# Forget rows of the prompt on partitions 0-15 and 64-79, the bias of each pair's odd head contracted over the second set (hybrid RG-LRU, forgetting attention, MoE step)

## The chip, the cores and the metric

One core of a Trainium2 chip runs the whole layer. The metric is device time in microseconds (us) of one execution; the time given is the median of several runs.

## The reference

One step of a decoder layer for two groups of tokens that share the weights: a prompt of 256 tokens and 8 samples of 8 new tokens, each with 256 cached ones. D = 1024, 16 heads of 64, 32 experts, all in fp32.

```
h   = rms_norm(x, g_mix_pre) * (1 + scale1) + shift1        # from c, by w_ada
z   = h @ w_in  ->  x_rnn | q | k | v | f_logit(16) | gate_A | gate_B
A:  causal conv (width 4) -> RG-LRU (block-diagonal gates, scan)
B:  logf = log_sigmoid(f_logit + b_forget);  F = cumsum(logf)      # one row per head
    softmax(q k^T / 8 + F_t - F_s, causal) v
x  += gate1 * rms_norm((sigmoid(gate_A) * A + sigmoid(gate_B) * B) @ w_out)
x  += gate2 * rms_norm(top-4-of-32 SwiGLU experts(...))
```

Outputs are also k, v, logf and the states of both groups. In a softmax row F_t is a constant and falls out, so the kernel adds only -F_s, a row for each head, to the scores.

## The kernel before

It is written with semaphores by hand; each engine has its own list of instructions, in program order.

**Input projection (to about 261 us).** TensorE runs JOBS in order: one job is a block of 128 output rows over all 320 tokens (kinds x, k, v, q, and the gates gb and ga), 8 matmuls over D (L1343), with weights from a staging ring of three chunks of 2 MB. An fp32 matmul shows as two instructions in the trace, so a job is x16. The kinds r and i are the block-diagonal gates (L1338). Kind a is a piece of the adaLN product, in column tiles of 32 (L1326), and a later fold (L1298) adds its four parts up, one job behind. ScalarE evacuates each job (job_ev).

The forget job, kind f, stands between the x and the k jobs. Its weights `wf` (1024 x 16 values) and bias `bfg` are loaded by SP among the small loads (L344, L345), between chunks 6 and 7; its 8 matmuls (L1331) give 16 rows of logits. ScalarE adds the bias (L562), VectorE and ScalarE make log-sigmoid in place (L834 on, `log1p`), a scan along the 256 tokens and a factor -1 give `Fp`, 16 partitions x 256 (L854, L855), and F_made is raised.

**Prompt attention (261 to 378 us).** Heads go in pairs p, 2p on partitions 0-63 and 2p+1 on 64-127 of qT and kT. `scores(p)` writes for two query blocks (128 and 256 keys) the q.k products of both heads (L1387), and adds the bias (L1390): the stationary operand is a column of the identity, broadcast to 128 columns over 16 partitions, which picks head h's row out of `Fp`. The four banks are used as two pairs.

```
for o in range(2):
    row = ident[0:H, 2 * p + o:2 * p + o + 1].to_broadcast([H, 128])
    last = mm(B[2 * (p % 2) + o][:, c:c + n], row, Fp[:, 0:n], start=False, stop=True)
```

TensorE's order is scores(0), scores(1), and then for each p: gate job 2p (L1370, 16 instructions), values(p-1) (L1408, L1411), weights(2p) (three transposes, L1235), gate job 2p+1, weights(2p+1), scores(p+2). VectorE takes the masked maximum and normalizes (L890 to L900), ScalarE does the exponentials (L588, L589).

**Samples and the middle (378 to 535 us).** For each of 8 samples cached keys and values come in (SP, L362), their keys are transposed, and scores and values are made; between them lie output projection, second norm and router.

**Experts (535 us to the end).** 16 pairs of experts; each takes 16 MB of gate-up (L399) and 8 MB of down weights (L403), streamed by SP as the semaphore `used`, which TensorE counts up, frees the slots. The first two transfers wait for the count that TensorE adds ahead of the last two samples (L1575 in the profile).

POOL zeroes and makes masks at the start (L420 to L441), and issues output transfers later.

Of the kernel before, what the change touches and what calls it, by code (L numbers as in the profile page):

```python
# [31 lines left out]
def hybrid_layer(nc, x_prompt, x_sample, cache_k, cache_v, cache_logf, state_conv, state_h, page_table,  # L32
# [11 lines left out]
    NT = D // 128  # L44
# [23 lines left out]
    with ctx:  # L68
# [36 lines left out]
        lfc = fr[:, 2432:2688].rearrange("p (g h) -> p g h", h=H)  # L105
        wf = fr[:, 2688:2816].rearrange("p (k h) -> p k h", h=H)
        onesf = fr[:, 2816:2816 + PAST + DS]
        st36 = fr[:, 3080:3080 + NT * 36].rearrange("p (t c) -> p t c", c=36)
        rs = fr[:, 3368:3688]
        lfcf, lftf = fr[:, 2432:2432 + 272], fr[:, 4008:4096]  # L110
        lfz = fr[0:H, 3688:4008]
        lftok = fr[:, 4008:4056].rearrange("p (t h) -> p t h", h=H)
# [95 lines left out]
        h2S = hf[:, 2048:2560].rearrange("p (m n) -> p m n", m=4)  # L208
        Fp = rs[0:H, 0:SP_]
        Fs = fr[:, 0:2 * (PAST + DS)].rearrange("p (s c) -> p s c", s=2)  # L210
# [5 lines left out]
        sp8, t8, s8, a8 = few(0, 8), few(8, 8), few(16, 8), few(24, 8)  # L216
        bfg = few(32, 1, H)
        brow = few(33, E, 1)
# [24 lines left out]
        def vec(name, n=NT):  # L243
            return vecT[:, V[name]:V[name] + n]


        names = """fold8_made fold_ps silu_zeroed tailk_made sv_ps sv_made smask8_made qsel_made hsel_made smask_made consts_made ident_made x_in rows_in small_in pages_in cachef_in rgw_zeroed rgw_in
            rows_ps vec_made csig_made c_made xT_ps xT_made xT_sq sum_ps ms_made rs_made ada_ps h_made
# [67 lines left out]
        def _(eng):  # L316
# [26 lines left out]
            eng.dma_start(ptab, page_table.rearrange("(o b) g -> o (b g)", o=1)).then_inc(s["pages_in"], 16)  # L343
            eng.dma_start(wf, winv[:, :, FCOL:FCOL + H]).then_inc(s["small_in"], 16)  # L344
            eng.dma_start(bfg, b_forget.rearrange("o h -> h o")).then_inc(s["small_in"], 16)  # L345
            eng.dma_start(wr[:, :, :].rearrange("p (h k) e -> p h k e", h=2), w_router[0].rearrange("(h p k) e -> p h k e", h=2, k=4)).then_inc(s["small_in"], 16)
            eng.dma_start(brow, b_router).then_inc(s["small_in"], 16)
            eng.wait_ge(s["rgw_zeroed"], 1)
            for g, w in enumerate((rg_w_a, rg_w_x)):
# [68 lines left out]
        def _(eng):  # L418
# [5 lines left out]
            eng.memset(silu_c, 0.0).then_inc(s["silu_zeroed"], 1)  # L424
            eng.memset(wax, 0.0).then_inc(s["rgw_zeroed"], 1)

            link(eng.memset(mask, 0.0))
            for o in (0, 256):
# [8 lines left out]
                              pattern=[[-1, 2 * NS - DS]], channel_multiplier=1).then_inc(s["smask8_made"], 1)  # L437
            eng.memset(onesf, 1.0).then_inc(s["consts_made"], 1)
            eng.memset(fr[:, 4008:4096], 0.0).then_inc(s["consts_made"], 1)
            eng.memset(xp[:, :, 0:CW - 1], 0.0).then_inc(s["xp_edges"], 1)  # L440
# [79 lines left out]
        def _(eng):  # L520
# [19 lines left out]
            def job(j):  # L540
# [3 lines left out]
                if kind == "a":  # L544
                    if t >= 4:
                        eng.wait_ge(s["fold_ps"], t - 3)
                    A_(adarow[:, t % 4, :], ps[:, :], ACT.Copy).then_inc(s["job_ev"], 1)
                elif kind == "v":
                    A_(gbT[:, t, :], ps[:, 0:T], ACT.Copy).then_inc(s["job_ev"], 1)  # L549
                elif kind == "k":  # L550
                    A_(kT[:, t, :], ps[:, 0:T], ACT.Copy).then_inc(s["job_ev"], 1)
                elif kind == "q":
                    if t == 0:
                        eng.wait_ge(s["fold_ps"], 12)
                    A_(qT[:, t, :], ps[:, 0:T], ACT.Copy, scale=SCALE).then_inc(s["job_ev"], 1)
                elif kind == "x":
                    link(A_(xp[:, t, CW - 1:CW - 1 + SP_], ps[:, 0:SP_], ACT.Copy))
                    A_(windows(xp, S0 + CW - 1, DS)[:, t, :, :], ps[:, SP_:T].rearrange("p (b q) -> p b q", q=DS),
                       ACT.Copy).then_inc(s["job_ev"], 1)
                elif kind == "f":  # L560
                    eng.wait_ge(s["small_in"], 64)
                    A_(lfz, ps[0:H, 0:T], ACT.Identity, bias=bfg).then_inc(s["job_ev"], 1)  # L562
                elif kind in ("r", "i"):
                    A_((R if kind == "r" else U)[:, t, :], ps[:, 0:OW], ACT.Tanh, scale=0.5,
                       bias=vec("rg_b_a" if kind == "r" else "rg_b_x")[:, t:t + 1]).then_inc(s["job_ev"], 1)
                else:
                    if kind == "gb" and t == 0:
                        eng.wait_ge(s["tr_ps"], G_ST)
                    A_((gaT if kind == "ga" else gbT)[:, t, :], B[4 + t % 2][:, 0:T], ACT.Tanh, scale=0.5).then_inc(s["job_ev"], 1)

            for j in range(GATES):
                job(j)
                if j == LAST["f"]:
                    eng.wait_ge(s["absw_made"], 2)
                    A_(lft[0:H, 0, 0:T], lft[0:H, 0, 0:T], ACT.Exp, scale=-1.0).then_inc(s["expw_made"], 1)
                if j == LAST["i"] - 1:
# [133 lines left out]
        def _(eng):  # L710
# [122 lines left out]

            w_, t_, x_ = lft[0:H, 1, 0:T], lft[0:H, 0, 0:T], lft[0:H, 2, 0:T]  # L834
            eng.wait_ge(s["job_ev"], LAST["f"])
# [7 lines left out]
            eng.wait_ge(s["expw_made"], 2)  # L843
            acc_ = PTs[0:H, 0, 0:T]
            log1p(acc_, t_, x_, w_, 1)
            link(TS(lfz, lfz, 0.0, None, ALU.min))
            STT(lfz, acc_, -2.0, lfz, ALU.mult, ALU.add).then_inc(s["lf_made"], 1)
            for g in range(4):
                q = 32 * g
                V_.tensor_copy(hsel[q:q + H, :].rearrange("k (h c) -> k h c", c=DS),  # L850
                               ident[q:q + H, q:q + H].unsqueeze(2).to_broadcast([H, H, DS])).then_inc(s["hsel_made"], 1)
            eng.wait_ge(s["consts_made"], 5)
            eng.wait_ge(s["lf_made"], 1)
            link(V_.tensor_tensor_scan(Fp, onesf[0:H, 0:SP_], lfz[:, 0:SP_], 0.0, ALU.mult, ALU.add))  # L854
            TS(Fp, Fp, -1.0, None, ALU.mult).then_inc(s["F_made"], 1)  # L855
# [210 lines left out]
            def constants():  # L1066
                eng.wait_ge(s["consts_made"], 5)
                link(V_.tensor_copy(steps, steps_i))
# [162 lines left out]
        def _(eng):  # L1231
# [42 lines left out]
            def transposes(g):  # L1274
# [8 lines left out]
                elif g == G_LF:  # L1283
                    eng.wait_ge(s["lf_made"], 1)
                    for k in range(TT):
                        last = tr(ps[0:TROWS[k], H * k:H * k + H], lfz[:, 128 * k:128 * k + TROWS[k]], H)
                else:
# [20 lines left out]
            for j, (kind, t) in enumerate(JOBS[:GATES]):  # L1308
# [19 lines left out]
                elif kind == "f":  # L1328
                    eng.wait_ge(s["small_in"], 64)
                    for k in range(NT):  # L1330
                        last = mm(ps[0:H, 0:T], wf[:, k, :], hT[:, k, :], start=(k == 0), stop=(k == NT - 1))  # L1331
                    last.then_inc(s["job_ps"], 1)
# [47 lines left out]
            def scores(p):  # L1380
# [3 lines left out]
                for c, q, n in ((0, 0, 128), (128, 128, 256)):  # L1384
# [3 lines left out]
                    for o in range(2):  # L1388
                        row = ident[0:H, 2 * p + o:2 * p + o + 1].to_broadcast([H, 128])
                        last = mm(B[2 * (p % 2) + o][:, c:c + n], row, Fp[:, 0:n], start=False, stop=True)  # L1390
                        if c:
# [154 lines left out]

            def router_of_prompt():
                eng.wait_ge(s["h2T_made"], 4)
                for k in range(2):
# [236 lines left out]
```

## Time and profile before

| | us |
|---|---|
| median of 3 runs (1498.5 to 1501.39) | 1500.78 |
| the profiled execution's own time | 1496.86 |
| its span in the profile | 1495.1 |
| TensorE (PE) busy | 1401.9 (94%) |
| VectorE (DVE) busy | 341.5 (23%) |
| ScalarE (ACT) busy | 232.1 (16%) |
| GpSimd (POOL) busy | 25.3 (2%) |
| mean granted TensorE clock | 0.96 of full |

The page divides the span into 40 slices of 37.4 us. PE is the matmuls, PEld the weight loads that overlap them, SPq the issuing of SP's transfers. A busy share is an average over stages with different limits; the chain of waits tells in each stage what the end hangs on. The granted clock has two levels, 1.2 GHz (0.5) and 2.4 GHz (1.0); a figure between them is a mean over a stretch.

### The profile page before, as it was taken

How to read it: one execution, taken by the hardware profiler on the slowest of the kernel's cores; microseconds unless marked ns; L12 is line 12 of the kernel's file. 1: busy time of each engine (PE TensorE's matmuls, PEld its weight loads, DVE VectorE, ACT ScalarE, POOL GpSimd, SP SyncE). 2: the span in 40 equal slices, each digit the busy share in tenths (PEclk: the TensorE clock that was granted, in tenths of full speed). 3: DMA queues.
4: the chain of work that ended last, by engine and by line, in shares of the span. 5: the costliest groups of instructions: out<-in, count | busy, mean ns of one | idle time of the engine just before them, and what ended most of it. 6: DMA issues, size and time to landing. Idle time of an engine off the chain costs nothing.

```text
span 1495.1 us, 15980 instructions
## 1 busy us (share of the span) xinstructions
PE 1401.9 (94%) x6379; PEld 641.1 (43%) x6379; DVE 341.5 (23%) x693; ACT 232.1 (16%) x461; POOL 25.3 (2%) x55
## 2 busy tenths in 40 slices
PE   6899899999989899999999999999999999999996
PEld 2555446666546344333333343333333433433432
DVE  3441321324334311211111021012110220121114
ACT  2011500322334201101011011010010110110102
POOL 1100000000100100000000000000000000000000
PEclk9899899999988789999999999999999999999998
DMA  8745364231334949999999999999999999999992
GB/s 294 224 173 212 106 220 160 106 148 57 121 113 141 367 167 418 430 428 427 428 427 427 426 420 429 429 427 427 426 426 428 427 428 412 426 430 428 427 427 107
DMA packets 68253, 483.67 MB, mean 323 GB/s; under 512 B 10238, under 2 KB 10982, under 8 KB 43605
## 3 DMA queue, kind: packets, MB, share of 16 engines
q1 hardware_dynamic: 66500, 477.69, 77.8%
q0 software_dynamic: 1680, 4.91, 1.0%
q8 instruction: 58, 0.95, 0.3%
q14 instruction: 15, 0.12, 0.0%
HBM read 478.48 MB, written 4.10 MB: 323 GB/s over the span
## 4 chain that ended last, share of the span: by engine, by line
PE 78%; DMA 16%; issue 2%; ACT 2%; DVE 2%; SPq 1%; DVEq 0%; ACTq 0%; PEldq 0%
PE bank L1700 36%; DMA ring<-in_w_gate_up_dram 15%; PE bank L1343 9%; PE bank L1370 5%; PE bank L1665 5%; PE bank L1235 4%; PE bank L1688 3%; PE bank L1666 3%; PE bank L1534 2%; PE bank L1326 2%; PE bank L1491 1%; PE bank L1390 1%; PE bank L1338 1%; PE bank L1325 1%; PE bank L1387 1%
## 5 line engine op out<-in xcount | busy, mean ns | idle before, releaser
L1700 PE MATMUL bank<-ring,work 128*64 128x512 f32 x2048 | 457.4, 600 | 16.1 <-issue 10.9
L1700 PEld LDWEIGHTS bank<-ring,work 128*64 128x64 f32 x2048 | 160.8, 138 | 290.5 <-issue 290.3
L1700 PE MATMUL bank<-ring,hT 128*64 128x512 f32 x1024 | 233.8, 603 | 15.8 <-DMA ring<-in_w_gate_up_dram 15.8
L1212 DVE TENSOR_TENSOR gbT<-gbT,bank 128x512 f32<-128x512 f32 x85 | 58.5, 688 | 453.1 <-PE bank L1688 392.5
L1343 PE MATMUL bank<-hT,ring 128*128 128x320 f32 x512 | 143.6, 441 | 5.7 <-DVEq L786 4.9
L1700 PEld LDWEIGHTS bank<-ring,hT 128*64 128x64 f32 x1024 | 77.0, 138 | 161.2 <-issue 161.2
L1343 PEld LDWEIGHTS bank<-hT,ring 128*128 128x128 f32 x512 | 98.0, 193 | 53.2 <-issue 6.9
L1181 DVE TENSOR_SCALAR work<-bank 128x512 f32<-128x512 f32 x32 | 22.0, 686 | 321.6 <-PE bank L1700 321.6
L1370 PE MATMUL bank<-hT,ring 128*128 128x320 f32 x256 | 75.5, 450 | 0.0
L1665 PE MATMUL bank<-qT,tok 128*128 128x256 f32 x256 | 72.4, 405 | 0.0
L688 ACT ACTIVATE work<-bank 128x320 f32<-128x320 f32 x16 | 7.0, 437 | 411.3 <-PE bank L1235 411.3
L1688 PE MATMUL bank<-work 128*128 128x512 f32 x136 | 67.4, 619 | 1.2 <-ACT work L700 1.2
L1370 PEld LDWEIGHTS bank<-hT,ring 128*128 128x128 f32 x256 | 49.3, 198 | 21.7 <-issue 4.8
L1665 PEld LDWEIGHTS bank<-qT,tok 128*128 128x128 f32 x256 | 43.5, 189 | 32.1 <-issue 28.9
L1235 PE MATMUL bank<-ident,work 128*128 128x128 f32 (+3 forms) x253 | 44.7, 298 | 11.6 <-DMA work<-in_state_conv_dram 10.4
L700 ACT ACTIVATE work<-bank 128x512 f32<-128x512 f32 x32 | 17.4, 594 | 217.6 <-PE bank L1700 217.6
L1235 PEld LDWEIGHTS bank<-ident,work 128*128 128x128 f32 (+3 forms) x253 | 30.7, 177 | 38.0 <-issue 36.7
L691 ACT ACTIVATE work<-work 128x512 f32<-128x512 f32 x32 | 20.2, 630 | 164.4 <-DVE work L1181 164.4
L1666 PE MATMUL bank<-qT,tok 64*128 64x256 f32 x128 | 44.6, 428 | 0.0
L1688 PEld LDWEIGHTS bank<-work 128*128 128x128 f32 x136 | 23.0, 189 | 45.3 <-issue 41.9
L1326 PE MATMUL bank<-ring 128*32 128x512 f32 x192 | 29.5, 706 | 13.4 <-ACT gbT L549 6.9
L1235 PE MATMUL bank<-ident,ring 128*128 128x128 f32 (+2 forms) x139 | 24.8, 338 | 6.8 <-ACT work L607 5.0
(335 smaller groups left out, 914.0 us busy)
## 6 DMA issues: line engine op xcount, KB each, us to landing
ring<-in_w_gate_up_dram SPq DMA_DIRECT2D x128, 2048.0 KB, 14.9
ring<-in_w_down_dram SPq DMA_DIRECT2D x64, 2048.0 KB, 16.9
ring<-in_w_ada_dram SPq DMA_DIRECT2D x12, 2048.0 KB, 8.0
ring<-in_w_in_dram SPq DMA_DIRECT2D x12, 2048.0 KB, 9.8
ring<-in_cache_k_dram SPq DMA_DIRECT2D x16, 512.0 KB, 6.9
ring<-in_cache_v_dram SPq DMA_DIRECT2D x16, 512.0 KB, 4.3
ring<-in_w_out_dram SPq DMA_DIRECT2D x2, 2048.0 KB, 7.6
out_dram<-tok POOLq DMA_DIRECT2D x2, 1024.0 KB, 5.2
```

Of the source, the lines that this page charges most:

```text
L691: A_(sig[:, 512 * j:512 * j + 512], glu[:, 512 * j:512 * j + 512], ACT.Sigmoid, scale=ALPHA)\
L1181: TS(glu[:, half[j]], B[j][:, :], LIMIT, None, ALU.min).then_inc(s["glu_made"], 1)
L1212: TTo(piece(gbf, n), piece(gbf, n), B[6 + n % 2][:, :], ALU.add).then_inc(s["scatter_read"], 1)
L1235: return nc.tensor.transpose(out, in_, ident[0:rows, 0:rows])
L1326: last = mm(ps[32 * g:32 * g + 32, :], silu_c[:, k, :], w[0][:, k, :], start=(k < 4), stop=(k >= 4))
L1343: last = mm(ps[:, 0:T], w[0][:, k, 128 * (t % 4):128 * (t % 4) + 128], hT[:, k, :], start=(k == 0), stop=(k == NT - 1))
L1370: last = mm(B[4 + h % 2][:, 0:T], w[0][:, k, 128 * (h % 4):128 * (h % 4) + 128], hT[:, k, :], start=(k == 0), stop=(k == NT - 1))
L1534: last = mm(B[5 + t][:, :], gaT[:, k, 128 * t:128 * t + 128], w[h][:, k, :], start=(k == 0), stop=(k == NT - 1))
L1665: mm(out, tok[:, k, 128 * m:128 * m + 128], sel[:, k, :], start=(k == 0), stop=False)
L1666: last = mm(out, tok[q:q + 64, 2, 128 * (m % 4):128 * (m % 4) + 128], sel[q:q + 64, 2, :], start=False, stop=True)
L1688: last = mm(bank[:, :], C[:, 128 * k:128 * k + 128], Ysb[:, 512 * (n % 2):512 * (n % 2) + 512], start=True, stop=True)
L1700: last = mm(bank[CAP * x:CAP * x + CAP, :], lhsT[:, CAP * x:CAP * x + CAP], rhs(x), start=start, stop=stop)
```

## The change

1. `wf` is 80 columns for each of the 8 blocks of D, and lies at another place of the same ring unit; columns 0-15 and 64-79 are the 16 weight columns, twice, and the rest is zero. `bfg` likewise. So the forget job gives logits on partitions 0-15 and 64-79.
2. Everything up to `Fp` runs on 80 partitions in place of 16. The transposes that write logf out take partitions 0-15.
3. The bias of the even head contracts over partitions 0-15, that of the odd one over 64-79.
4. POOL zeroes `wf` (128x640) and `bfg`, and 16 columns behind the cached log-forget values. SP issues the small loads of the router first, then waits for all of POOL's zeroing, then issues weights and bias of the forget job twice. A semaphore of their own, forget_in, tells of them; the router waits for small_in.

```diff
         lfc = fr[:, 2432:2688].rearrange("p (g h) -> p g h", h=H)
-        wf = fr[:, 2688:2816].rearrange("p (k h) -> p k h", h=H)
+        H2 = 64 + H
+        wf = fr[:, 0:NT * H2].rearrange("p (k h) -> p k h", h=H2)
         onesf = fr[:, 2816:2816 + PAST + DS]
...
         lfcf, lftf = fr[:, 2432:2432 + 272], fr[:, 4008:4096]
-        lfz = fr[0:H, 3688:4008]
+        lfz = fr[0:H2, 3688:4008]
         lftok = fr[:, 4008:4056].rearrange("p (t h) -> p t h", h=H)
...
         h2S = hf[:, 2048:2560].rearrange("p (m n) -> p m n", m=4)
-        Fp = rs[0:H, 0:SP_]
+        Fp = rs[0:H2, 0:SP_]
         Fs = fr[:, 0:2 * (PAST + DS)].rearrange("p (s c) -> p s c", s=2)
...
             eng.dma_start(ptab, page_table.rearrange("(o b) g -> o (b g)", o=1)).then_inc(s["pages_in"], 16)
-            eng.dma_start(wf, winv[:, :, FCOL:FCOL + H]).then_inc(s["small_in"], 16)
-            eng.dma_start(bfg, b_forget.rearrange("o h -> h o")).then_inc(s["small_in"], 16)
             eng.dma_start(wr[:, :, :].rearrange("p (h k) e -> p h k e", h=2), w_router[0].rearrange("(h p k) e -> p h k e", h=2, k=4)).then_inc(s["small_in"], 16)
             eng.dma_start(brow, b_router).then_inc(s["small_in"], 16)
-            eng.wait_ge(s["rgw_zeroed"], 1)
+            eng.wait_ge(s["rgw_zeroed"], 3)
+            for two in range(2):
+                o = 64 * two
+                eng.dma_start(wf[:, :, o:o + H], winv[:, :, FCOL:FCOL + H]).then_inc(s["forget_in"], 16)
+                eng.dma_start(bfg[o:o + H, :], b_forget.rearrange("o h -> h o")).then_inc(s["forget_in"], 16)
             for g, w in enumerate((rg_w_a, rg_w_x)):
...
             eng.memset(wax, 0.0).then_inc(s["rgw_zeroed"], 1)
+            eng.memset(wf, 0.0).then_inc(s["rgw_zeroed"], 1)
+            eng.memset(bfg, 0.0).then_inc(s["rgw_zeroed"], 1)
 
...
             eng.memset(onesf, 1.0).then_inc(s["consts_made"], 1)
+            eng.memset(fr[:, 2688:2704], 0.0).then_inc(s["consts_made"], 1)
             eng.memset(fr[:, 4008:4096], 0.0).then_inc(s["consts_made"], 1)
...
                 elif kind == "f":
-                    eng.wait_ge(s["small_in"], 64)
-                    A_(lfz, ps[0:H, 0:T], ACT.Identity, bias=bfg).then_inc(s["job_ev"], 1)
+                    eng.wait_ge(s["forget_in"], 64)
+                    A_(lfz, ps[0:H2, 0:T], ACT.Identity, bias=bfg).then_inc(s["job_ev"], 1)
                 elif kind in ("r", "i"):
...
 
-            w_, t_, x_ = lft[0:H, 1, 0:T], lft[0:H, 0, 0:T], lft[0:H, 2, 0:T]
+            w_, t_, x_ = lft[0:H2, 1, 0:T], lft[0:H2, 0, 0:T], lft[0:H2, 2, 0:T]
             eng.wait_ge(s["job_ev"], LAST["f"])
...
                                ident[q:q + H, q:q + H].unsqueeze(2).to_broadcast([H, H, DS])).then_inc(s["hsel_made"], 1)
-            eng.wait_ge(s["consts_made"], 5)
+            eng.wait_ge(s["consts_made"], 6)
             eng.wait_ge(s["lf_made"], 1)
-            link(V_.tensor_tensor_scan(Fp, onesf[0:H, 0:SP_], lfz[:, 0:SP_], 0.0, ALU.mult, ALU.add))
+            link(V_.tensor_tensor_scan(Fp, onesf[0:H2, 0:SP_], lfz[:, 0:SP_], 0.0, ALU.mult, ALU.add))
             TS(Fp, Fp, -1.0, None, ALU.mult).then_inc(s["F_made"], 1)
...
                     for k in range(TT):
-                        last = tr(ps[0:TROWS[k], H * k:H * k + H], lfz[:, 128 * k:128 * k + TROWS[k]], H)
+                        last = tr(ps[0:TROWS[k], H * k:H * k + H], lfz[0:H, 128 * k:128 * k + TROWS[k]], H)
                 else:
...
                 elif kind == "f":
-                    eng.wait_ge(s["small_in"], 64)
+                    eng.wait_ge(s["forget_in"], 64)
                     for k in range(NT):
-                        last = mm(ps[0:H, 0:T], wf[:, k, :], hT[:, k, :], start=(k == 0), stop=(k == NT - 1))
+                        last = mm(ps[0:H2, 0:T], wf[:, k, :], hT[:, k, :], start=(k == 0), stop=(k == NT - 1))
                     last.then_inc(s["job_ps"], 1)
...
                     for o in range(2):
-                        row = ident[0:H, 2 * p + o:2 * p + o + 1].to_broadcast([H, 128])
-                        last = mm(B[2 * (p % 2) + o][:, c:c + n], row, Fp[:, 0:n], start=False, stop=True)
+                        d, h = slice(64 * o, 64 * o + H), 64 * o + 2 * p + o
+                        last = mm(B[2 * (p % 2) + o][:, c:c + n], ident[d, h:h + 1].to_broadcast([H, 128]), Fp[d, 0:n], start=False, stop=True)
                         if c:
...
             def router_of_prompt():
+                eng.wait_ge(s["small_in"], 32)
                 eng.wait_ge(s["h2T_made"], 4)
...
```

**SP, the small loads between chunk 6 and chunk 7.** Here is the program before:

```order
L339 DMA ring<-in_w_in_dram 128x8x512 [waits chunk_free]
L343 DMA tiny<-in_page_table_dram 1x16
L344 DMA ring<-in_w_in_dram 128x8x16
L345 DMA tiny<-in_b_forget_dram 16x1
L346 DMA wr<-in_w_router_dram 128x2x128
L347 DMA tiny<-in_b_router_dram 1x32
L353 DMA ring<-in_rg_w_a_dram 64x8x64 [waits rgw_zeroed]
L353 DMA ring<-in_rg_w_a_dram 64x8x64
L353 DMA ring<-in_rg_w_x_dram 64x8x64 x2
L339 DMA ring<-in_w_ada_dram 128x8x512 [waits chunk_free]
```

and the change:

```order
L340 DMA ring<-in_w_in_dram 128x8x512 [waits chunk_free]
L344 DMA tiny<-in_page_table_dram 1x16
L345 DMA wr<-in_w_router_dram 128x2x128
L346 DMA tiny<-in_b_router_dram 1x32
L350 DMA ring<-in_w_in_dram 128x8x16 [waits rgw_zeroed]
L351 DMA tiny<-in_b_forget_dram 16x1
L350 DMA ring<-in_w_in_dram 128x8x16
L351 DMA tiny<-in_b_forget_dram 16x1
L356 DMA ring<-in_rg_w_a_dram 64x8x64 x2
L356 DMA ring<-in_rg_w_x_dram 64x8x64 x2
L340 DMA ring<-in_w_ada_dram 128x8x512 [waits chunk_free]
```

Two more transfers lie between chunk 6 and chunk 7, and the wait for POOL's zeroing stands four transfers earlier.

**TensorE, the forget job and its neighbours** (L1326 and L1325 are a job of kind a, L1298 its fold, L1343 the first k job), before:

```order
L1325 MATMUL bank<-xT,ident 32x512
L1326 MATMUL bank<-ring 32x512 x4
L1331 MATMUL bank<-hT,ring 16x320 [waits job_ps,small_in,job_ev]
L1331 MATMUL bank<-hT,ring 16x320 x7
L1298 MATMUL bank<-qT,fold 32x512 [waits job_ev]
L1343 MATMUL bank<-hT,ring 128x320 [waits chunk_in2,job_ev]
```

and the change:

```order
L1331 MATMUL bank<-xT,ident 32x512
L1332 MATMUL bank<-ring 32x512 x4
L1337 MATMUL bank<-hT,ring 80x320 [waits job_ps,forget_in,job_ev]
L1337 MATMUL bank<-hT,ring 80x320 x7
L1304 MATMUL bank<-qT,fold 32x512 [waits job_ev]
L1349 MATMUL bank<-hT,ring 128x320 [waits chunk_in2,job_ev]
```

The order is the same; the job's output is 80 rows in place of 16, and it waits for the new semaphore.

## Rows read from the trace of the kernel before

**Rows 1.** Busy tenths of TensorE in 40 slices, and GB/s moved in each.
```profile
PE   6899899999989899999999999999999999999996
...
GB/s 294 224 173 212 106 220 160 106 148 57 121 113 141 367 167 418 430 428 427 428 427 427 426 420 429 429 427 427 426 426 428 427 428 412 426 430 428 427 427 107
```
**Rows 2.** The chain that ended last: shares by engine and by line.
```profile
PE 78%; DMA 16%; issue 2%; ACT 2%; DVE 2%; SPq 1%; DVEq 0%; ACTq 0%; PEldq 0%
PE bank L1700 36%; DMA ring<-in_w_gate_up_dram 15%; PE bank L1343 9%; PE bank L1370 5%; PE bank L1665 5%; PE bank L1235 4%; PE bank L1688 3%; PE bank L1666 3%; PE bank L1534 2%; PE bank L1326 2%; PE bank L1491 1%; PE bank L1390 1%; PE bank 
```
**Rows 3.** Chain in order of time, 264 to 283 us: start us, us, what.
```profile
264.30 0.42 PE bank L1387 x4
264.72 0.94 PE bank L1390 x4
265.66 1.16 PE bank L1387 x4
266.81 2.00 PE bank L1390 x4
268.81 5.97 PE bank L1370 x16
...
279.75 0.42 PE bank L1387 x4
280.17 0.64 PE bank L1390 x4
280.81 0.63 PE bank L1387 x4
281.44 1.05 PE bank L1390 x4
```
**Rows 4.** Stretches: busy us of PE, PEld, DVE, ACT, POOL; PEclk, DMA share, GB/s.
```profile
264.70:268.70 4.00, 4.00 (x14) 2.33 (x12) 2.34 (x7) 2.19 (x8) 0.00 (x0) 0.53 0.90 345
293.00:376.00 83.00, 82.39 (x394) 55.46 (x394) 29.80 (x95) 21.38 (x64) 0.61 (x1) 0.98 0.31 114
58.00:68.00 10.00, 10.00 (x38) 6.82 (x36) 4.62 (x9) 1.23 (x4) 0.00 (x0) 1.00 0.00 0
```
**Rows 5.** Chain in order of time, 70 to 100 us.
```profile
71.76 4.54 PE bank L1343 x16
...
77.28 13.13 PE bank L1343 x48
...
94.07 3.66 PE bank L1331 x13
...
98.53 1.54 PE bank L1343 x5
```
**Rows 6.** POOL's timeline (start us, us), and TensorE's longest wait in 0 to 20.
```profile
1.89 1.80 POOL L425 MEMSET ring<- 128x2048 f32 x1
...
PE bank L1235 <- DMA work<-in_state_conv_dram: 10.4, 1, 10.4
```
**Rows 7.** Timeline of SP's issues, 39 to 72 us.
```profile
42.40 1.63 SPq L344 DMA_DIRECT2D ring<-in_w_in_dram  x1
44.07 5.29 SPq L345 DMA_DIRECT2D tiny<-in_b_forget_dram  x1
...
53.03 1.31 SPq L353 DMA_DIRECT2D ring<-in_rg_w_x_dram  x2
68.21 0.37 SPq L339 DMA_DIRECT2D ring<-in_w_ada_dram  x1
```
**Rows 8.** SP from 485 us: an issue, and a wait (us, times, longest).
```profile
489.87 20.52 SPq L399 DMA_DIRECT2D ring<-in_w_gate_up_dram  x6
...
SPq L399 <- PEq L1575: 1.0, 1, 1.0
```
**Rows 9.** Chain in order of time: two gate jobs, behind two score groups.
```profile
296.15 4.50 PE bank L1370 x16
...
322.98 6.19 PE bank L1370 x16
```

More of the change, by code:

```diff
@@ L216, in hybrid_layer @@
         sp8, t8, s8, a8 = few(0, 8), few(8, 8), few(16, 8), few(24, 8)
-        bfg = few(32, 1, H)
+        bfg = few(32, 1, H2)
         brow = few(33, E, 1)
@@ L244, in vec @@
             return vecT[:, V[name]:V[name] + n]
-        names = """fold8_made fold_ps silu_zeroed tailk_made sv_ps sv_made smask8_made qsel_made hsel_made smask_made consts_made ident_made x_in rows_in small_in pages_in cachef_in rgw_zeroed rgw_in
+        names = """fold8_made fold_ps silu_zeroed tailk_made sv_ps sv_made smask8_made qsel_made hsel_made smask_made consts_made ident_made x_in rows_in small_in forget_in pages_in cachef_in rgw_zeroed rgw_in
             rows_ps vec_made csig_made c_made xT_ps xT_made xT_sq sum_ps ms_made rs_made ada_ps h_made
@@ L574, in _ @@
                     eng.wait_ge(s["absw_made"], 2)
-                    A_(lft[0:H, 0, 0:T], lft[0:H, 0, 0:T], ACT.Exp, scale=-1.0).then_inc(s["expw_made"], 1)
+                    A_(lft[0:H2, 0, 0:T], lft[0:H2, 0, 0:T], ACT.Exp, scale=-1.0).then_inc(s["expw_made"], 1)
                 if j == LAST["i"] - 1:
@@ L843, in _ @@
             eng.wait_ge(s["expw_made"], 2)
-            acc_ = PTs[0:H, 0, 0:T]
+            acc_ = PTs[0:H2, 0, 0:T]
             log1p(acc_, t_, x_, w_, 1)
@@ L1066, in constants @@
             def constants():
-                eng.wait_ge(s["consts_made"], 5)
+                eng.wait_ge(s["consts_made"], 6)
                 link(V_.tensor_copy(steps, steps_i))
```

## The prediction

> **What bounds the kernel now.** I read the page's slices first, then the chain of waits, then stretches of it in order of time. The slices show two regimes [rows 1]. From the 16th slice on the DMA engines are at their limit (412 to 430 GB/s in every slice but the last); these are the expert pairs. Before that, TensorE is at 8 or 9 tenths in nearly all slices and the transfers are not dense. The chain says the same: PE 78%, DMA 16%, and nearly all of the DMA share is the gate-up weights [rows 2]. So there are two questions: does this edit shorten TensorE's path before that, and does what it saves there reach the start of the expert weights' stream?
>
> The part of the chain to look at is prompt attention. One pair's scores are four groups in a row, all TensorE, without a gap: q.k over 128 keys 0.42 us, bias 0.64, q.k over 256 keys 0.63, bias 1.05, and then the gate job [rows 3]. The reader is to see that bias and q.k have the same count (x4) and the same moving sizes, and that the bias takes longer. The two heads' q.k matmuls lie on partitions 0-63 and 64-127, in two banks; the two heads' bias matmuls both lie on partitions 0-15. From 293 to 376 us TensorE is busy 82.39 of 83 us [rows 4], so time taken from a score group is taken from the path.
>
> **The change part by part.**
>
> *Bias matmuls.* Their number stays. The odd head's moves to partitions 64-79, as its q.k already does. The nearest row for "same moving size, two halves of the array, two banks" is L1387 in the same pair: so 0.64 should become 0.42 and 1.05 should become 0.63, which is 0.22 + 0.42 = 0.64 us a pair. Pair 0 and the six pairs after pair 1 show these lengths to 0.02 us; one stands in the rows. Pair 1 ran partly at the lower granted clock (mean 0.53 from 264.7 to 268.7, so mostly at 1.2 GHz [rows 4]): its bias groups took 0.94 and 2.00, its q.k groups 0.42 and 1.16 [rows 3]. If the low stretch stays tied to this pair, it saves 2.94 - 1.58 = 1.36, and all eight save 7 x 0.64 + 1.36 = 5.84. If instead the low stretch lasts as long as before, whatever work falls in it, the saving is 8 x 0.64 = 5.12. I take the middle, 5.5, since nothing in one trace tells them apart; both ends go into the range.
>
> The Trainium skill ("TensorE: Matmul & The Clock Gate", Part 3, the mechanism) says that a weight load overlaps running matmuls only where its row group differs, and that tiles side by side cost one matmul's duration plus some 4 ns for each further tile. By that rule taken as it stands a bias group would halve, (0.64 + 1.05) / 2 = 0.85 us a pair and 6.8 for eight; the whole would then be -5.7, or 1495.1. The L1387 groups, which are two such tiles already, are longer than half of the bias groups, so the trace speaks for the smaller gain.
>
> *The forget job (eight matmuls in two passes, 16 instructions).* Its stationary operand grows from 16 to 80 columns. From the job's start to the next job's, with the two L1298 matmuls of the fold in it, it takes 98.53 - 94.07 = 4.46 us [rows 5]. A 128-column job of the same moving size with such a fold behind it takes 77.28 - 71.76 = 5.52 [rows 5]. The difference is the fold, which runs beside the 16-column job (32 other columns) and behind the 128-column one. For 80 columns I take the second, the nearer in width and the one whose columns meet the fold's. That is +1.06 us on the path. The other bound is 0, if the overlap stays. The Trainium skill speaks against this part of the change too ("TensorEngine Tiling (Array Packing)", Key Properties: a change of tiling mode drains the array): by it this job leaves the mode of its neighbours and pays two drains, which the page does not price. The 128-column job with its fold, by which the sum goes, holds such changes already [rows 5].
>
> *Weights and bias of the forget job, loaded twice.* SP issues two more small DMAs and waits for POOL's zeroing. POOL: zeroing 128x2048 took 1.80 us and ended at 3.7 [rows 6]; a further 128x640 is 0.6 us at that rate, with some 0.2 for the small ones, right behind it and long before SP comes to that point at 42 us. TensorE's first instruction waits 10.4 us for a DMA [rows 6], so POOL's later mask costs it nothing. SP: the two issues took 1.63 and 5.29 us, the block ends at 54.3, and SP's next issue is at 68.21, when a chunk comes free [rows 7]. 6.9 us more make it 61.3, still 7 us early. The transfers: from 58 to 68 us the DMA engines move nothing [rows 4], and 64 KB more, a thirty-second of a chunk, fit in there. Its consumer is the forget job at 94.07. Queued behind on SP are the block-diagonal weights, for jobs that come later than the forget job. If this cover were gone, the first to suffer would be the chunk issued at 68.21, which is used once the jobs of 77.28 have run their 13.13 us, at 90.4: 22 us of room. Cost 0.
>
> *Elementwise work on 80 partitions in place of 16* (log-sigmoid, scan, exp): the same elements in each partition, so the same time; the chain there is TensorE alone [rows 5]. The new zeroing of 16 columns lies with POOL's others, and the router's added wait is for loads that SP issued before 54.3 us: 0.
>
> **The carry.** Behind attention come the samples' heads, whose cached keys and values SP fetches when TensorE's counts free their buffers, so that part shifts whole. SP issues the first gate-up transfer at 489.87, after a wait for TensorE's count (L1575) [rows 8]; nothing there is tied to an absolute time. From the 16th slice on the stream runs at its limit [rows 1], so it starts earlier and ends earlier by what TensorE saved, and loses nothing of it.
>
> **The sum.** -5.5 + 1.1 = -4.4 us. The profiled execution took 1496.86 (span 1495.1), 3.9 below the median shown, so it would come to 1492.5; against the median of 1500.78 it is **1496.4 us**. A measurement of this kernel can tell some 0.2% (3.0 us) from no change, so this is faster, by a small margin.
>
> **Rivals.**
>
> 1. *The low clock goes.* In attention the granted clock falls twice: after the two score groups in a row (pair 1 lost 0.30 + 0.53 + 0.95 against the usual groups, and the job behind it took 5.97 in place of 4.50: 3.25 us together [rows 3, 9]), and after the scores at 320 (6.19 in place of 4.50: 1.69 us [rows 9]). Both follow groups that use few rows of the array. The first burst, pairs 0 and 1, gets shorter by 2 us. If that fall stays away, the path loses 5.12 + 3.25 - 1.06 = 7.3 us: 1493.5; with both gone 9.0: 1491.8. For: where the falls lie. Against: four of the same groups in between had none, so it is partly chance.
>
> 2. *No overlap.* Two 16-row matmuls side by side occur nowhere in this trace, only 64-row ones. If the hardware or the lowering keeps them one behind the other, the edit doesn't do what it says, and only the forget job is left: +1.1, so 1501.9. Against it: all that L1387 has (other partitions, other bank) the bias would have too.
>
> 3. *Absorbed.* TensorE's saving turns into waits, either for the softmax of the next heads or at the hand-over to the weights' stream. Then it is 0 to +1.1: 1500.8 to 1501.9. Against: TensorE has 0.6 us of idle time in 83 [rows 4], and the stream's gates are TensorE's own counts [rows 8].
>
> 4. *Slower: the clock falls after more score groups.* If two 16-row matmuls side by side keep the clock up less well than one behind the other did, the falls spread to the other score groups. The one at 320 us costs 1.69 us; the five other groups behind pair 1 that have none would add 8.5, so 1496.4 + 8.5 = 1504.9. It decides the sign from three further falls on (5.1 against 4.4), and it is slower by 0.2% from five on (8.5 - 4.4 = 4.1). For: falls do follow these groups. Against: the groups get shorter, and full-size jobs follow at once.
>
> **How the numbers follow.** Forecast 0.60, of which some 0.06 comes out within 0.2% by scatter (runs of one kernel lie 2.9 us apart); low clock gone 0.16; no overlap 0.09; absorbed 0.09; slower 0.06. Faster by over 0.2%: 0.54 + 0.16 = 0.70. Within: 0.06 + 0.18 = 0.24. Slower: 0.06. The forecast's own range is -5.84 + 0 to -5.12 + 1.06, so 1494.9 to 1496.7, with 1.5 us of scatter on either side. Downward the whole range takes in the clock rival (1493.5, and 1491.8 with both falls gone); upward it stops at 1500.0, where 0.8 of the 4.4 us are left, and leaves out most of rivals 2 to 4. So 1491.5 to 1500.0.
>
> **What would show it.** Bias groups of 0.42 and 0.63 us in the chain, a pair's scores 2.1 in place of 2.74; the forget job 5.5 us to the next one; SP's block over before 62; the first gate-up issue near 485.5; the last 25 slices at the same GB/s as before. Bias groups of 0.64 and 1.05 make me wrong in the first step, an unmoved gate-up issue in the carry, and a low clock in other places of the first 540 us in the size.

## The result and the profile after

| | before | after |
|---|---|---|
| median of 8 runs, us | 1500.05 | 1489.34 |
| lowest to highest | 1497.12 to 1502.17 | 1488.17 to 1494.81 |
| span of the profiled execution | 1495.1 | 1487.4 |

The ratio is 0.9925, 95% interval 0.9909 to 0.994: faster by 0.75%, 10.7 us between the medians. The forecast was 1496.4 (4.4 us), its range ended at 1491.5, so the gain is more than twice the one forecast and lies outside the range. The profiled executions differ by 7.7 us. The one of the kernel before took 1496.86 us, 3.2 below its median, that of the change 1489.11, 0.2 below; that makes up the 3.0 us between 7.7 and 10.7.

The page of the changed kernel, lines of 1, 2 (the granted clock in tenths) and 4:

```profile
PE 1392.1 (94%) x6379; PEld 632.8 (43%) x6379; DVE 339.3 (23%) x693; ACT 231.8 (16%) x461; POOL 26.1 (2%) x58
...
PEclk9899989999988799999999999999999999999998
...
PE 76%; DMA 18%; ACT 2%; issue 2%; DVE 1%; SPq 1%; DVEq 0%; ACTq 0%; PEldq 0%
```

What answers to [rows 3], the chain in order of time (start us, us, what; L1393 is q.k, L1396 the bias, L1376 the gate job):

```profile
265.46 0.42 PE bank L1393 x4
265.88 0.42 PE bank L1396 x4
266.30 0.63 PE bank L1393 x4
266.94 0.63 PE bank L1396 x4
267.57 4.50 PE bank L1376 x16
...
277.04 0.42 PE bank L1393 x4
277.46 0.42 PE bank L1396 x4
277.88 0.63 PE bank L1393 x4
278.51 0.63 PE bank L1396 x4
```

Every bias group now takes 0.42 or 0.63 us, as long as these q.k groups of its size, as the step said. What the step did not say: pair 1 and the gate job behind it are at full speed too (4.50 where [rows 3] has 5.97). And what answers to the two clock rows: in the whole of 260 to 370 us the granted clock is 1.00; before it was 0.95 (columns as in [rows 4]).

```profile
260.00:370.00 110.00, 108.37 (x546) 71.70 (x545) 41.03 (x128) 33.59 (x99) 1.11 (x2) 1.00 0.29 106
```

```profile
260.00:370.00 110.00, 108.68 (x495) 72.14 (x495) 36.65 (x115) 32.61 (x96) 0.61 (x1) 0.95 0.29 106
```

The forget job with its fold, as in [rows 5] (L1337 the job, L1304 the fold, L1349 the next job):

```profile
93.69 4.50 PE bank L1337 x16
98.19 0.98 PE bank L1304 x2
99.17 1.01 PE bank L1349 x3
```

99.17 - 93.69 = 5.48 us where [rows 5] has 4.46: nothing is mixed any more, the fold stands behind the job. SP's block of small loads, as in [rows 7]:

```profile
49.86 0.43 SPq L350 DMA_DIRECT2D ring<-in_w_in_dram  x1
50.33 3.20 SPq L351 DMA_DIRECT2D tiny<-in_b_forget_dram  x1
...
54.96 1.31 SPq L356 DMA_DIRECT2D ring<-in_rg_w_x_dram  x2
67.80 0.37 SPq L340 DMA_DIRECT2D ring<-in_w_ada_dram  x1
```

It ends at 56.3, more than 11 us before the next chunk's issue.

**Where the time went.** I cut the span at three instructions: the first score matmul, the first transpose of the cached log-forget values behind the attention loop (L1422 before, L1428 after), and the first expert matmul (535.4 and 527.8 us). The view of one line gives duration ns min/median/max, then the first and last start:

```profile
L1422 PE MATMUL bank<-ident,ring x32: 272/273/297, 367.4 to 371.9; 128*32 128x128 f32 x32
```

```profile
L1428 PE MATMUL bank<-ident,ring x32: 272/273/297, 359.2 to 363.6; 128*32 128x128 f32 x32
```

| stretch | before | after | difference |
|---|---|---|---|
| start to the first score matmul | 261.5 | 263.3 | +1.8 |
| attention loop | 105.9 | 95.9 | -10.0 |
| samples, output, router | 168.0 | 168.6 | +0.6 |
| experts to the end of the span | 959.7 | 959.6 | -0.1 |

The -10.0 of the attention loop is 8 x 0.64 = 5.12 of shorter bias groups, 3.25 for the low clock around pair 1 and 1.69 for the one at 320 us, which sum to 10.06. In the start, 1.0 of the 1.8 us is the forget job; the other stretches are looked at below, under the last 2 us. So I have the terms; whether the second and third belong to the change or to this one execution is what the runs had to tell.

### The profile page after: what moved, and what is told of

It reads as the page before. It is cut to its first block, busy times and chain, and to the rows that moved or that the text cites. A ratio compares the mean times of both kernels' runs of the same rounds, so it can differ in the third digit from the quotient of the medians.

```text
span 1487.4 us, 15986 instructions
## 1 busy us (share of the span) xinstructions
PE 1392.1 (94%) x6379; PEld 632.8 (43%) x6379; DVE 339.3 (23%) x693; ACT 231.8 (16%) x461; POOL 26.1 (2%) x58
## 4 chain that ended last, share of the span: by engine, by line
PE 76%; DMA 18%; ACT 2%; issue 2%; DVE 1%; SPq 1%; DVEq 0%; ACTq 0%; PEldq 0%
PE bank L1707 35%; DMA ring<-in_w_gate_up_dram 16%; PE bank L1349 9%; PE bank L1376 5%; PE bank L1672 5%; PE bank L1241 4%; PE bank L1695 3%; PE bank L1673 3%; PE bank L1540 2%; PE bank L1332 1%; PE bank L1497 1%; PE bank L1344 1%; PE bank L1609 1%; PE bank L1627 1%; PE bank L1393 1%
## 5 line engine op out<-in xcount | busy, mean ns | idle before, releaser
L1349 PE MATMUL bank<-hT,ring 128*128 128x320 f32 x512 | 144.3, 442 | 5.7 <-DVEq L792 4.9
L1349 PEld LDWEIGHTS bank<-hT,ring 128*128 128x128 f32 x512 | 98.3, 194 | 54.4 <-issue 7.1
L1376 PE MATMUL bank<-hT,ring 128*128 128x320 f32 x256 | 72.4, 436 | 0.0
L1376 PEld LDWEIGHTS bank<-hT,ring 128*128 128x128 f32 x256 | 47.4, 190 | 20.1 <-issue 2.3
```

Of the source, the lines that this page charges most:

```text
L1349: last = mm(ps[:, 0:T], w[0][:, k, 128 * (t % 4):128 * (t % 4) + 128], hT[:, k, :], start=(k == 0), stop=(k == NT - 1))
L1376: last = mm(B[4 + h % 2][:, 0:T], w[0][:, k, 128 * (h % 4):128 * (h % 4) + 128], hT[:, k, :], start=(k == 0), stop=(k == NT - 1))
```

## The experiments

The theories. **A**: the bias side by side saves 5.1 us of work, and because TensorE then spends less time in a row on matmuls that use few rows, the granted clock stays up and gives some 5 us more. **B**: the falls of the clock come at times that have nothing to do with what runs; or part of the gain comes from another edit.

### e1: the bias back on one set

```diff
-    d, h = slice(64 * o, 64 * o + H), 64 * o + 2 * p + o
-    last = mm(..., ident[d, h:h + 1].to_broadcast([H, 128]), Fp[d, 0:n], ...)
+    row = ident[0:H, 2 * p + o:2 * p + o + 1].to_broadcast([H, 128])
+    last = mm(..., row, Fp[0:H, 0:n], ...)
```

> The change with both heads' bias again over partitions 0-15 (forget job still 80 columns, double load kept). Theory A (the overlap of the bias matmuls saves 5.1 us of work, and the shorter score groups keep the granted clock up, which gives the rest of the 10.7): all of the gain goes, bias groups 0.64 and 1.05 us, a low clock behind the first two score groups again, time 1.0 us above the kernel before, about 1501. Rival B (part of the gain comes from the other edits, such as the order of SP's small loads or the shift of the work against the clock): the time stays clearly below before, 1494 to 1498, with the bias groups long.

Measured: 1500.19 us against 1498.98 before, ratio 0.9996 (0.9977 to 1.0015). Everything else of the change stands in this kernel, and no gain is left. In the chain the clock is low again from the second of the first two groups on, in nearly the same figures as [rows 3]:

```profile
266.06 1.15 PE bank L1393 x4
267.21 2.00 PE bank L1396 x4
269.21 6.21 PE bank L1376 x16
...
283.13 4.50 PE bank L1376 x16
```

A second fall lies at 296 us, behind a single score group, another one than before. The loop takes 105.9 us. The gain comes with the bias part; rival B's second half is out.

### e2: narrow forget rows

```diff
+    eng.dma_start(wf, winv[:, :, FCOL:FCOL + H])            # once, 16 wide
...
-    last = mm(ps[0:H2, 0:T], wf[:, k, :], hT[:, k, :], ...)
+    for o in (0, 64):
+        last = mm(ps[o:o + H, 0:T], wf[:, k, :], hT[:, k, :], ...)
```

> The change, but the forget rows are made by two matmuls of 16 columns each, into output partitions 0-15 and 64-79, with wf loaded once and 16 wide. Theory: two narrow column tiles run side by side and beside the fold, so the forget job and its fold take 4.4 to 4.5 us again in place of 5.5, and the kernel is 1.0 us below the change, 1488.3; the bias part is untouched. Rival: the 16-column matmuls don't overlap each other, then the job takes 8.6 us and the kernel is 3 us above the change, 1492.5.

Measured: ratio 0.9931 (0.9906 to 0.9956), 1491.33 us. From the forget job to the next job:

```profile
98.40 3.68 PE bank L1337 x26
102.08 0.19 PE bank L1303
102.27 0.08 PE bank L1337 x2
...
102.89 3.16 PE bank L1349 x11
```

102.89 - 98.40 = 4.49 us: twice as many matmuls in the time that one narrow set took before, mixed with the fold (L1303). The mechanism and its 1.0 us are as expected; the total can't show 1 us, since the interval of the ratio is 7.5 us wide, and the change itself was timed in another comparison. The 1.0 us that the wide job costs is thus no price of having two sets, only of the 80 columns.

### e3: the first two score groups apart

```diff
     scores(0)
-    scores(1)
     for p in range(NT):
         gate_job(2 * p)
+        if p == 0:
+            scores(1)
```

(in the kernel before; VectorE's list has the norms of heads 0 and 1 ahead of the maxima of 2 and 3)

> The kernel before, bias as it was; only the second score group is moved behind the first gate job (and VectorE normalizes heads 0 and 1 before the maxima of 2 and 3). It keeps every matmul. Theory A (the clock falls because two score groups stand in a row): no low clock in 261 to 280 us, both groups at 2.74 us, 3.2 us less less a possible wait of weights(0), so 1497 to 1498. Rival B (the falls come by chance of time, not by what runs): no change within 1 us, 1500, with a fall in attention still seen.

Measured: ratio 0.9977 (0.9954 to 1.0), the loop 104.5 us. Chain:

```profile
268.43 4.50 PE bank L1375 x16
...
274.62 1.05 PE bank L1395 x4
...
276.15 4.31 PE bank L1375 x16
...
283.54 6.20 PE bank L1375 x16
...
298.89 4.50 PE bank L1375 x16
```

The fall behind the first groups is gone (4.50, and 1.05 for the bias of pair 1). But the gate job at 283.54, behind a single score group, takes 6.20, and there is another such fall at 352 us. So the first fall goes with the two groups in a row, and behind single groups of the old length there are shorter ones now and then. Theory A is half confirmed: it named the place, but the loop got only 1.4 us shorter in place of 3.2, since this profile has two single falls (1.7 us each) where the one before had one.

### e4: the work put back as full-size matmuls

```diff
+    if h % 2 == 0:
+        mm(B[4 + h % 2][:, 0:T], w[0][:, 0, ...], hT[:, 0, :], start=True, stop=True)
     for k in range(NT):
```

> The change with one more full-size matmul (two instructions, 0.55 us, its result overwritten) ahead of every second gate job, eight in all: 4.4 us of full-array work in place of most of the 5.1 saved. Theory A (short, dense score groups keep the clock): the clock stays up in attention, and the kernel is 4.4 us above the change, 1493.7, so still 6 below before. Rival B (the falls only came with the position in time): falls come back in attention in the profile, 1496 to 1499.

Measured: ratio 0.9934 (0.9907 to 0.9961), 1491.58 us, so 7.4 below before; I had expected 4.4 above the change and got 2.2, between medians of two comparisons and inside the intervals. The profile is clearer than the time:

```profile
271.94 4.31 PE bank L1378 x16
...
284.05 4.31 PE bank L1378 x16
```

The loop takes 100.2 us, 4.3 more than the change's 95.9, as much as was put in, and the clock never falls in it. Against the loop of before (105.9) it is 5.7 us shorter: 0.8 of that is work (5.1 taken out, 4.3 put in), and 4.9 is the two falls of the clock that are not there.

### e5 and e8: second profiles of both kernels

> The kernel before once more, for a second profile. Theory A (serial bias groups let the clock fall): from the first score group to the cached log-forget transposes 105 to 107 us, with falls behind the first two groups and some single one. Rival B (chance): the stage lies anywhere from 101 (no fall) on, and the falls have gone.

> The change once more, for a second profile and a ratio on this chip. Theory A: no fall in attention again, stage 95.8 to 96 us, ratio 0.992 to 0.994. Rival B: falls in attention in this profile, stage 98 to 101 us.

Measured: before, loop 104.3 us, again with a fall that begins in the second of the first two groups, none behind a single one:

```profile
270.78 1.74 PE bank L1390 x4
272.51 7.16 PE bank L1370 x16
```

That is just under the 105 to 107 expected, which had a single fall in it. The change: loop 95.9, no fall, ratio 0.9954 (0.9929 to 0.998), outside the 0.992 to 0.994 expected. So the gain in this comparison is 8.6 us between the medians, smaller than the first 10.7; the intervals overlap.

### e6: full rows, no side by side

```diff
-    row = ident[0:H, 2 * p + o:2 * p + o + 1].to_broadcast([H, 128])
-    last = mm(..., row, Fp[:, 0:n], ...)
+    row = ident[:, 2 * p + o:2 * p + o + 1].to_broadcast([128, 128])
+    last = mm(..., row, rs[:, 0:n], ...)
```

(in the kernel before; the other rows of rs meet zeros of the identity)

> The kernel before with the bias contracted over all 128 partitions (one-hot column over the whole identity, and the whole of rs in place of its first 16 rows), still one head behind the other. Bias groups stay 0.64 and 1.05 us. Theory A1 (the clock counts how many rows of the array the matmuls use): no falls in attention, the stage from scores to cached log-forget is 101 us, time 5 us below before, 1494. Theory A2 (what counts is how long the score group is, or the drains in it, whatever the rows): falls as before, 105.9 us, 1499.

Measured: ratio 0.9966 (0.9948 to 0.9985), 5.1 us below before on the medians. Chain:

```profile
268.19 0.64 PE bank L1390 x4
...
269.46 1.06 PE bank L1390 x4
270.52 4.31 PE bank L1370 x16
...
281.49 1.06 PE bank L1390 x4
282.55 4.31 PE bank L1370 x16
```

The bias groups are as long as before, 0.64 and 1.06, one head behind the other, and the clock does not fall, neither behind the two groups in a row nor later. The score groups take the same time; what differs is the rows of the array that the bias uses. This is the run that parts rows from length, and it says rows. It is one profile, and it can't part the number of rows from the size of the tile, which changes with it. A by-product: the gate job is 4.31 in place of 4.50, with a bias before it that already uses the whole array. Seven gate jobs stand right behind a bias group, and seven times 0.19 is 1.3 us, about the 1.2 by which the loop (99.8) beats the 101 that I expected. The Trainium skill ("TensorEngine Tiling (Array Packing)", Key Properties) has a drain at each change of tiling mode; the trace agrees, with 0.19 us for the change that is left out here.

### e7: the bias side by side, twice

```diff
-    for o in range(2):
+    for i in range(4):
+        o = i % 2
```

(in the change, with -F/2 in place of -F)

> The change with -F/2 in place of -F and the bias added twice, each time both heads side by side: a score group is 2.1 + 0.42 + 0.63 = 3.15 us, longer than the 2.74 of before, but as dense as the change's. Theory A1 (density or rows used count): no falls in attention, stage 95.9 + 8.4 = 104.3 us. Theory A2 (length of the group counts): falls come back, the stage is 106 to 110 us, and the time 1499 or more.

Measured: ratio 0.9991 (0.9973 to 1.001), the loop 104.4 us. Chain:

```profile
270.02 0.64 PE bank L1397 x8
...
271.30 1.65 PE bank L1397 x8
272.95 7.25 PE bank L1376 x16
...
286.86 1.06 PE bank L1397 x8
287.92 4.50 PE bank L1376 x16
```

The expectation mis-sized the groups: a second bias adds 0.22 and 0.43 us, not 0.42 and 0.63, since about 0.2 us of a group is there once, however many matmuls follow. So a pair's scores are 2.75 us, the length of before, with twice the bias matmuls in them. The fall behind the first two is back (1.65 in place of 1.06, and 7.25 in place of 4.50: 3.3 us), and there is none behind single groups. That the loop of 104.4 meets the 104.3 that theory A1 gave for "no falls" is luck, the sum of two errors: 8 x 0.65 of work and 3.3 of clock on 95.9. So packing two 16-row matmuls side by side does not keep the clock up as such. Together with e6 this says that the change keeps it up by making the stretch of few rows shorter (the first two groups 4.3 us in place of 7.3, or of 5.5 at full clock); it rests on one profile of each.

### e9 and e10: half the array for each head

```diff
-    d, h = slice(64 * o, 64 * o + H), 64 * o + 2 * p + o
-    last = mm(..., ident[d, h:h + 1].to_broadcast([H, 128]), Fp[d, 0:n], ...)
+    d, h = slice(64 * o, 64 * o + 64), 64 * o + 2 * p + o
+    last = mm(..., ident[d, h:h + 1].to_broadcast([64, 128]), rs[d, 0:n], ...)
```

> The change with each head's bias contracted over its whole half of the array (64 rows of the identity's column and of rs, in place of 16), so bias and q.k use the same tiles. From e6 (gate jobs behind a full-row bias 4.31 in place of 4.50) a switch between tile sizes costs 0.1 to 0.2 us. Theory: bias groups lose their switches, 0.42 to about 0.3 and 0.63 to about 0.5, and so do the q.k groups; a score group takes 1.4 to 1.6 us in place of 2.1, eight of them save 4 to 5 us; no falls; stage 91 to 92 us, time 4 to 5 us below the change. Rival: the switch cost is not between 64 and 16 rows but a plain cost of changing banks, then the groups stay at 2.1 and the stage at 95.9.

> As e9, with the forget rows from two narrow column tiles as in e2. Theory: stage from scores to cached log-forget as in e9, and the forget job with its fold 4.5 us in place of 5.5, so 1.0 us below e9: 1484 to 1486 where before is 1500. Rival: the two don't add (the time is that of e9 within its interval and the forget job is 5.5).

Measured: e9 1486.76 us, ratio 0.99 (0.988 to 0.992), loop 91.3; e10 1485.0 us, ratio 0.9878 (0.9855 to 0.9901), loop 91.2. Chain of e9:

```profile
265.37 0.45 PE bank L1396 x4
265.83 0.55 DVE work L896
...
271.70 0.55 PE bank L1241 x3
272.24 4.31 PE bank L1376 x16
...
277.52 0.43 PE bank L1393 x4
277.96 0.43 PE bank L1396 x4
278.39 4.50 PE bank L1376 x16
```

Bias and q.k have the same tiles now, and three of the four groups of a pair lose 0.2 us each; from 276.88 to 278.39 a pair's scores take 1.5 us, where the change has 2.1. At the start the chain goes over VectorE's maxima (265.83) and comes back with the transposes at 271.70: the softmax of the first heads is now ready no earlier than TensorE, whose gate job ends at 271.62. It costs next to nothing yet. From the first score matmul to these transposes it is 7.5 us (264.22 to 271.70) where the change has 8.8 (263.29 to 272.07), and the transposes take 0.55 in place of 0.33. A further saving in these first groups would probably be lost to the softmax; that was not tried. Both are faster than the kernel before. Neither was timed beside the change: e10's interval lies below both of the change's, e9's touches the first of them, and the loops say 4.6 us for both. Of the kernels here e10 has the lowest ratio. Its forget job with the fold takes 4.5 us in its trace, as in e2, but 1.8 us between two medians of six runs prove no 1.0.

**All attention loops in one place.**

| profile | a pair's scores, us | rows of a bias matmul | falls behind the first two / single groups | loop, us |
|---|---|---|---|---|
| before | 2.74 | 16 | 1 / 1 | 105.9 |
| before, again (e5) | 2.74 | 16 | 1 / 0 | 104.3 |
| e1 | 2.74 | 16 | 1 / 1 | 105.9 |
| e3 | 2.74 | 16 | apart / 2 | 104.5 |
| e7 | 2.75 | 16, side by side, twice | 1 / 0 | 104.4 |
| e6 | 2.75 | 128 | 0 / 0 | 99.8 |
| after | 2.10 | 16, side by side | 0 / 0 | 95.9 |
| after, again (e8) | 2.10 | 16, side by side | 0 / 0 | 95.9 |
| e2 | 2.10 | 16, side by side | 0 / 0 | 95.8 |
| e4 | 2.10 | 16, side by side | 0 / 0 | 100.2 |
| e9 | 1.50 | 64, side by side | 0 / 0 | 91.3 |
| e10 | 1.50 | 64, side by side | 0 / 0 | 91.2 |

The loops are differences of starts given to 0.1 us, and the scores are at full clock. The four profiles with 16-row bias and 2.74 or 2.75 us of scores, two pairs in a row, have the first fall each time; the four with the change's groups have none, nor have e6, e9 and e10. Rival B, chance of time, does not explain that.

## Why the prediction was wrong

- **Bias matmuls: right.** 0.22 + 0.42 a pair, measured to the hundredth; rival 2 (no overlap) is out. (The reading that pair 0 has the usual lengths to 0.02 us leaves out its first q.k group, which took 0.49 in place of 0.42; nothing rests on it.) The Trainium skill's span of one matmul plus some 4 ns for each further tile ("TensorE: Matmul & The Clock Gate", Part 3), worked out as half of 0.64 and 1.05, is an estimate of 0.32 and 0.53; the trace has 0.42 and 0.63, as the L1387 rows said. e7 and e9 show why: of 0.64 and 1.05 only 0.43 and 0.85 are matmuls, which do halve (to 0.22 and 0.43), and the 0.2 us at the change of tile size stays.
- **Forget job: right.** +1.06 forecast, +1.02 measured.
- **SP, POOL, the double loads, 80 partitions: right,** cost 0; the block ended at 56.3 where 61.3 was allowed for, because the two pairs of issues took 5.5 and 3.6 us and not 6.9 each. VectorE's operations of the log-sigmoid took 486 ns on 80 partitions where they had taken 479 on 16, which is off the path.
- **The carry: right.** 9.0 us less at the first gate-up issue would follow from loop and forget job; the profiles have 489.87 and 481.2, 8.7 less, and the experts take 959.7 and 959.6 us.
- **The clock: wrong, and this is the step that failed.** For pair 1 I weighed "the low stretch stays tied to this pair" against "it lasts as long as before", and took the middle. Both keep the fall. That the fall goes stood apart as rival 1 with 0.16, and the argument against it ("four of the same groups in between had none, so it is partly chance") mixed two things. It also miscounted: the chain has three such groups between the two falls (280, 293 and 307 us) and five in all without one. Behind single groups of the old length the fall is chancy: none, none, one and one in the four profiles that have six such places each, two in e3's eight. Behind the two in a row it came in each of the four. With the change the first is gone, which e1, e5 and e8 bear out. None of its four profiles has a single fall either, in 24 places where the rate of before, 4 in 32, would give three; that makes the second gain likely and not certain. The term was 0.4 us of clock; it measured 3.3 to 4.9.
- **Rival 4** did not come: in the change's four profiles no score group has a fall behind it. In e7, where a pair's scores are as long as before, the two pairs in a row have one, but no single pair has.
- **The last 2 us.** Rival 1 with both falls gone gave 1491.8; measured were 1489.3 in the first comparison and 1492.0 in the second (e8, where before was 1500.6). The loops and the forget job give 9.0 us between the first two profiles and 7.4 between e5 and e8. The other stretches scatter by as much as what is missing. From the loop to the experts: 168.0, 170.5, 171.3 and 170.3 us with the old bias (before, e5, e1, e3), 168.2 in e6, 167.6 in e7, 168.1 to 168.7 in the change's four, but 169.1 and 170.0 in e9 and e10. The granted clock of this stretch is 0.84 or 0.85 in the first four and 0.86 in both profiles of the change, but 0.84 goes with 168.0 as well as with 171.3; what makes this difference was not tried, and stays open. The experts take 959.6 to 963.4 us. The first score matmul comes anywhere from 261.5 to 267.3 us, with TensorE at a mean clock of 0.90 to 0.93 in the first 100 us: up to 264.2 us where the granted clock of the first 260 us is 0.94 or 0.95, from 264.9 on where it is 0.92 or 0.93. So this scatter goes with the clock, in kernels of both kinds; why the clock differs there is open too.

## What to carry to other kernels

Small contractions that stand in a row on the same rows of the array can be put on rows 0 and 64 and run side by side, if the operand is there twice; making it there twice cost 1.0 us here, and nothing that the trace shows (4.49 us against 4.46) when the two copies were made by narrow column tiles. Count a stretch of few-row matmuls twice: once for its length, and once for the granted clock behind it, and look at each place where that clock falls in the trace for what all such places have in common before calling it chance. If the other rows hold finite values, contract a one-hot operand over the whole tile that the neighbouring matmuls use: here it was as fast, saved the switch of 0.2 us, and no fall of the clock was seen.

## What was not expected of the hardware

- TensorE is hardly idle in the loop (82.39 of 83 us busy [rows 4]) and still falls to the low clock. The same sequence with 128 rows in place of 16 in the bias (e6) had no fall, so idle time is not what precedes it here.
- A 128-row bias matmul took the same time as a 16-row one (0.64 and 1.06), and the gate job behind it 0.19 us less.
- Doubling the matmuls of a side-by-side group added 0.22 us to 0.42 and 0.43 to 0.63 (e7): about 0.2 us of each such group is its switch, and e9, where bias and q.k have the same tiles, saved 0.6 us of 2.1 in each pair's scores.
- Matmuls on different columns of the array start out of program order. In the kernel before, the fold's two matmuls start at 97.30 and 97.75 us; matmuls of the forget job, which stands ahead of the fold in the program, start at 97.56 and from 97.83 us on.
